# 16x16 blocks of a head's triangular inverse on VectorE by way of DMA, in a new order of the head rounds

## What is computed

```python
kk = einsum('cd,sd->cs', k, k)
a_mat = where(tri_strict, beta[:, None] * kk * decay, 0.0)
sol = triangular_solve(a_mat + eye, concat([v * beta, k * (beta * exp(G))]), lower=True, unit_diagonal=True)
value, k_cum = sol[..., :dv], sol[..., dv:]
for each chunk:                       # a recurrence over the chunks
    v_new = value - k_cum @ s
    o = q_dec @ s + attn_intra @ v_new
    s = s * chunk_decay + k_dec.T @ v_new
```

## Time and profile before

| | us |
|---|---|
| three runs | 2012.69, 2012.9, 2009.73 (median 2012.69) |
| the profiled execution | 2013.07 |
| its span, first to last instruction | 2011.3 |
| TensorE busy | 1960.4 (97% of the span) |
| VectorE, ScalarE, GpSimd busy | 905.4, 688.3, 931.0 |
| granted clock of TensorE, mean | 0.994 |

### The profile page before, as it was taken

How to read it: one execution, slowest core, us unless ns; L and a number is a source line. 1 busy time by engine, 2 the same in 40 slices (tenths; PEclk the granted TensorE clock), 3 DMA queues, 4 the chain that set the end, 5 groups by cost and what they waited for, 6 DMA issues and landing times.

```text
span 2011.3 us, 28269 instructions
## 1 busy us (share of the span) xinstructions
PE 1960.4 (97%) x10421; PEld 1600.4 (80%) x10421; DVE 905.4 (45%) x1567; ACT 688.3 (34%) x1383; POOL 931.0 (46%) x711
## 2 busy tenths in 40 slices
PE   7899999999999999999999999999999999999997
PEld 5787778877787888888888788888778888888886
DVE  4766776677652222121212356576532234335143
ACT  4333333333342223332324344544422332222122
POOL 3443354434444456444445533234244565646455
PEclk9999999999999999999999999999999999999998
DMA  5122212222222342323323322112142323323222
GB/s 190 54 85 73 73 27 78 83 63 63 65 72 84 121 157 92 105 95 94 98 92 102 117 84 74 52 63 74 53 136 85 107 80 105 105 84 100 92 101 73
DMA packets 52902, 178.50 MB, mean 89 GB/s; under 512 B 6688, under 2 KB 7520, under 8 KB 52576
## 3 DMA queue, kind: packets, MB, share of 16 engines
q1 hardware_dynamic: 52336, 174.88, 26.9%
q10 hardware_dynamic: 496, 2.65, 0.4%
HBM read 173.29 MB, written 4.23 MB: 88 GB/s over the span
## 4 chain that ended last, share of the span: by engine, by line
PE 93%; DVE 4%; issue 1%; ACT 1%; DMA 0%; POOL 0%; POOLq 0%; DVEq 0%; SPq 0%; ACTq 0%
PE bank L286 27%; PE bank L288 26%; PE bank L287 26%; PE bank L1515 2%; PE bank L1504 2%; PE bank L1498 2%; PE bank L974 1%; PE bank L1691 1%; PE bank L1678 1%; PE bank L958 1%; PE bank L944 1%; PE bank L918 0%; DMA residual<-x_t 0%; DVE raw_z L1893 0%; PE bank L1555 0%
## 5 line engine op out<-in xcount | busy, mean ns | idle before, releaser
L275 POOL TENSOR_TENSOR slab_lo<-slab_raw,slab_hi 128x512 fp32r<-128x512 f32 x604 | 824.2, 1389 | 977.7 <-ACT slab_hi L268 977.6
L286 PE MATMUL bank<-u_hi,slab_hi 128*128 128x512 f32 x1584 | 658.3, 416 | 21.9 <-POOL slab_lo L275 13.8
L288 PE MATMUL bank<-u_hi,slab_lo 128*128 128x512 f32 x1584 | 621.2, 392 | 0.0
L287 PE MATMUL bank<-u_lo,slab_hi 128*128 128x512 f32 x1584 | 619.6, 391 | 0.0
L268 ACT CAST slab_hi<-slab_raw 128x1024 fp32r<-128x1024 f32 x302 | 314.0, 1045 | 224.4 <-PE bank L288 223.3
L286 PEld LDWEIGHTS bank<-u_hi,slab_hi 128*128 128x128 f32 x1584 | 299.1, 189 | 85.7 <-issue 23.4
L288 PEld LDWEIGHTS bank<-u_hi,slab_lo 128*128 128x128 f32 x1584 | 298.3, 188 | 65.1
L287 PEld LDWEIGHTS bank<-u_lo,slab_hi 128*128 128x128 f32 x1584 | 299.7, 189 | 53.7 <-issue 1.9
L286 PE MATMUL bank<-hidden_hi,slab_hi 128*128 128x512 f32 x432 | 168.4, 390 | 0.3
L288 PE MATMUL bank<-hidden_hi,slab_lo 128*128 128x512 f32 x432 | 168.1, 389 | 0.0
L287 PE MATMUL bank<-hidden_lo,slab_hi 128*128 128x512 f32 x432 | 168.1, 389 | 0.0
(11 more groups left out here) (340 smaller groups left out, 2626.3 us busy)
## 6 DMA issues: line engine op xcount, KB each, us to landing
slab_raw<-slabs SPq DMA_DIRECT2D x302, 512.0 KB, 3.5
g_and_cum_rows<-row_store SPq DMA_DIRECT2D x7, 512.0 KB, 6.3
residual<-x_t SPq DMA_DIRECT2D x2, 1024.0 KB, 7.2
x_tok<-x SPq DMA_DIRECT2D x1, 2048.0 KB, 12.5
residual<-x_t SPq DMA_DIRECT2D x1, 2048.0 KB, 9.0
residual_store<-residual SPq DMA_DIRECT2D x1, 2048.0 KB, 10.0
residual<-residual_store ACTq DMA_DIRECT2D x1, 2048.0 KB, 8.8
out_t<-residual SPq DMA_DIRECT2D x8, 256.0 KB, 2.0
```

Source lines behind the costliest of these rows:

```text
L275: ins = pool.tensor_tensor(w_lo[s][:, ks, :], raw[s][:, ks, :], w_hi[s][:, ks, :].bitcast(F32), ALU.subtract)
L286: pe.matmul(bank, w_hi[s][:, k, :], x_hi[:, k, :], start=first, stop=False)
L287: pe.matmul(bank, w_hi[s][:, k, :], x_lo[:, k, :], start=False, stop=False)
L288: mm = pe.matmul(bank, w_lo[s][:, k, :], x_hi[:, k, :], start=False, stop=last)
```

## The change

The inverse's first levels leave TensorE. After `kk`, SP stores the masked matrix `a_t` to DRAM (`blocks_out`) and loads the 32 diagonal blocks of 16x16 back, one to a partition (`sub_u`, 32 partitions by 256). VectorE inverts all 32 blocks at once: `zb1` does sizes 2 and 4 in a few instructions on 8 to 16 elements and joins them to 8 (`join(4)`), `zb2` joins to 16 (`join(8)`). A join is two small matrix products, each one multiplication over all terms and a sum over the last axis. SP then stores the inverted blocks to a DRAM buffer that was zeroed once and loads the 64-wide diagonal halves back to `zi` (`blocks_back`). Levels 16, 32 and the last one stay on TensorE (`Y0` to `Y2`, `X0` to `X2`). GpSimd makes the two level masks over full tiles in one place (`am`). The masks of `kk` become one instruction. `ORDER` is rewritten: `fr` ahead of s0.0, `kpd` early, `zb1` and `zb2` around `S1`, and the steps from `xt` on later by up to some ten slab parts.

```diff
-LEVELS = 7
+SB = 16
+SUBS = T // SB
+DIAG = SB * (SB + 1)
+LEVELS = (16, 32)
 HB, QB = 64, 32
 HW = NT * HB
 SCALE = float(P) ** -0.5
 SLOTS = 4
-DVE_STEPS, LATE_STEPS = 26, 10
+DVE_STEPS, LATE_STEPS = 38, 10
...
     row_view = row_store.rearrange("(a h n) t -> h a (n t)", a=2, h=HEADS)
+    pitch = (P // SB) * SB * (P + 1)
+    a_store, z_store = [nc.dram_tensor(f"{x}_blocks_store", (NT * pitch,), F32, kind="Internal").ap() for x in "az"]
+
+    def tiles_in(store):
+        return store.rearrange("(n x) -> n x", n=NT)[:, 0:P * P].rearrange("n (p c) -> p n c", p=P)
+
+    def blocks_in(store):
+        return store.rearrange("(q x) -> q x", q=SUBS)[:, 0:SB * P].rearrange("q (i w) -> q i w", w=P)[:, :, 0:SB]
+
...
         kp, kd, vp = head("k_rhs", [P, T]), head("k_dec", [P, T]), head("v_rhs", [P, T])
-        a_c, a_off = a_t[:, 0:HW], a_t[:, HW:T]
-        a_levels, inv_prod = head("a_levels", [P, T]), head("inv_and_prod", [P, T])
-        atm = [a_levels[:, 0:HW], a_levels[:, HW:T]]
+        inv_prod = head("inv_and_prod", [P, T])
+        atm = [head(f"a_level{b}", [P, T]) for b in LEVELS]
+        sub_u, sub_z = [head(n, [SUBS, DIAG]) for n in ("blocks_u", "blocks_z")]
+        sub_p, sub_w = junk[0:SUBS, :], head("blocks_sums", [SUBS, 64])
         xi, yi = inv_prod[:, 0:HW], inv_prod[:, HW:T]
...
 
-        ORDER = """fvt s0.0 dif s0.1 colb fr bd s0.2 eg fk s0.3 kk th3 s0.4 S0 s0.5 z0 s0.6 xt sl3 E0 s0.7 dm qk s1.0 Y1
-                   e0 s1.1 tv P0 s1.2 vp s1.3 s1.4 X1 kpd T0 S1 s1.5 E1 s1.6 Y2 qd P1 s1.7 O0 s2.0 X2 e1 T1 S2 s2.1
-                   E2 cv0.0 s2.2 Y3 O1 s2.3 cv0.1 P2 X3 s2.4 cv0.2 s2.5 Y4 T2 s2.6 S3 cv0.3 s2.7 X4 E3 s3.0 e2 O2 s3.1 Y5
-                   th0 P3 s3.2 cv1.0 s3.3 X5 T3 cv1.1 s3.4 sl0 s3.5 Y6 O3 cv1.2 s3.6 tq s3.7 X6 cv1.3 s4.0 e3 s4.1 vk
-                   th1 s4.2 s4.3 r0 sl1 s4.4 r1 tfq s4.5 v1 cv2.0 s4.6 s4.7 r2 tk s5.0 v2 e4 s5.1 cv2.1 s5.2 r3 tfk
-                   s5.3 v3 cv2.2 s5.4 osq cv2.3 s5.5 s5.6 s5.7 on th2 s6.0 e5 s6.1 ot sl2 s6.2 oa s6.3 cola s6.4 colh
-                   s6.5 s6.6 s6.7 e6""".split()
+        ORDER = """fvt fr s0.0 dif s0.1 colb bd s0.2 eg fk s0.3 kk th3 s0.4 S0 s0.5 am s0.6 kpd E0 s0.7 dm qk s1.0 e0
+                   s1.1 tv P0 s1.2 vp zb1 T0 S1 s1.3 s1.4 zb2 E1 P1 s1.5 s1.6 qd s1.7 O0 s2.0 e1 s2.1 sl3 s2.2 T1 S2 s2.3
+                   E2 cv0.0 s2.4 O1 s2.5 cv0.1 P2 xt s2.6 cv0.2 s2.7 T2 s3.0 S3 Y0 e2 s3.1 cv0.3 E3 O2 s3.2 X0 s3.3 th0
+                   P3 cv1.0 s3.4 Y1 s3.5 T3 cv1.1 s3.6 X1 sl0 s3.7 O3 cv1.2 s4.0 Y2 e3 s4.1 tq cv1.3 s4.2 X2 th1 s4.3
+                   s4.4 vk s4.5 tfq sl1 s4.6 r0 cv2.0 s4.7 r1 s5.0 v1 e4 s5.1 cv2.1 tk s5.2 r2 s5.3 v2 cv2.2 s5.4 tfk s5.5
+                   r3 cv2.3 s5.6 v3 s5.7 osq th2 s6.0 e5 s6.1 s6.2 on sl2 cola s6.3 colh s6.4 ot s6.5 oa s6.6 s6.7
+                   e6""".split()
         LATE = {"cv0.0", "cv0.1", "cv0.2", "cv0.3", "cv1.0", "cv1.1", "cv1.2", "cv1.3", "cv2.0", "cv2.1", "cv2.2",
                 "cv2.3", "th0", "th1", "th2", "sl0", "sl1", "sl2", "tq", "tfq", "tk", "tfk", "cola", "colh"}
...
+            def blocks_out(c):
+                sp.wait_ge(sem("masked"), c + 1)
+                sp.wait_ge(sem("blocks_moved"), 80 * c + 32)
+                sp.dma_start(tiles_in(a_store), c4(a_t[:])).then_inc(sem("blocks_moved"), 16)
+                sp.wait_ge(sem("blocks_moved"), 80 * c + 48)
+                sp.dma_start(sub_u[:, 0:SB * SB].rearrange("q (i j) -> q i j", j=SB), blocks_in(a_store))\
+                    .then_inc(sem("blocks_moved"), 16)
+
+            def blocks_back(c):
+                sp.wait_ge(sem("sub_z"), c + 1)
+                sp.dma_start(blocks_in(z_store), sub_z[:, 0:SB * SB].rearrange("q (i j) -> q i j", j=SB))\
+                    .then_inc(sem("blocks_moved"), 16)
+                sp.wait_ge(sem("blocks_moved"), 80 * c + 80)
+                for r in (0, HB):
+                    sp.dma_start(c4(zi[r:r + HB, :]), tiles_in(z_store)[r:r + HB, :, r:r + HB])\
+                        .then_inc(sem("blocks_moved"), 16)
+
+            sp.wait_ge(sem("mhalf"), 1)
+            sp.dma_start(z_store[0:P * T].rearrange("(p t) -> p t", t=T), zeros[:]).then_inc(sem("blocks_moved"), 16)
+            sp.dma_start(z_store[P * T:].rearrange("(p t) -> p t", t=T), zeros[0:1, :]).then_inc(sem("blocks_moved"), 16)
+
...
                             if ph is ph_heads and j == 5:
+                                blocks_out(i - 1)
+                            if ph is ph_heads and j == 6:
+                                blocks_back(i - 1)
                                 load_rows(i)
                 else:
                     for j in range(ph.n):
                         load_slab(sp, ph, start, j)
+                        if ph is ph_gates and j == 5:
+                            blocks_out(HEADS - 1)
+                        if ph is ph_gates and j == 6:
+                            blocks_back(HEADS - 1)
             for m in range(KT):
                 sp.wait_ge(sem("result"), m + 1)
...
                 def level_y(l):
-                    if l < LEVELS - 1:
-                        pe.wait_ge(sem("atm"), 6 * c + l + 1)
-                    if l == 1:
-                        pe.wait_ge(sem("x0"), c + 1)
-                    else:
-                        pe.wait_ge(sem("x_new"), 5 * c + l - 1)
-                    if l < LEVELS - 1:
-                        quads(bA, atm[l % 2], xi).then_inc(sem("y_ps"), 1)
-                        return
+                    if l < len(LEVELS):
+                        pe.wait_ge(sem("atm"), 2 * c + l + 1)
+                    pe.wait_ge(sem("x_new"), 3 * c + l + 1)
                     pe.sem_inc(sem("level_begun"), 1)
                     for n in range(NT):
                         q = slice(n * HB, (n + 1) * HB)
-                        mm = pe.matmul(bA[HI, q], a_off[LO, q], xi[LO, q], start=True, stop=True)
+                        if l < len(LEVELS):
+                            for r in (LO, HI):
+                                mm = pe.matmul(bA[r, q], atm[l][r, n * P + r.start:n * P + r.stop], xi[r, q],
+                                               start=True, stop=True)
+                        else:
+                            mm = pe.matmul(bA[HI, q], a_t[LO, n * P + HB:(n + 1) * P], xi[LO, q], start=True, stop=True)
                     mm.then_inc(sem("y_ps"), 1)
 
                 def level_x(l):
-                    pe.wait_ge(sem("y"), 6 * c + l)
-                    if l == 1:
+                    pe.wait_ge(sem("y"), 3 * c + l + 1)
+                    if l == 0:
                         pe.wait_ge(sem("v_rhs"), c + 1)
-                    if l > 1:
-                        pe.wait_ge(sem("z_new"), 6 * c + l - 1)
-                    if l < LEVELS - 1:
-                        quads(bC, yi, zi).then_inc(sem("zy_ps"), 1)
-                        return
+                    else:
+                        pe.wait_ge(sem("z_new"), 3 * c + l)
                     pe.sem_inc(sem("level_begun"), 1)
                     for n in range(NT):
-                        mm = pe.matmul(bC[LO, n * HB:(n + 1) * HB], yi[HI, n * HB:(n + 1) * HB],
-                                       zf[HI, n * P + HB:(n + 1) * P], start=True, stop=True)
+                        q = slice(n * HB, (n + 1) * HB)
+                        if l < len(LEVELS):
+                            for r in (LO, HI):
+                                mm = pe.matmul(bC[r, q], yi[r, q], zi[r, q], start=True, stop=True)
+                        else:
+                            mm = pe.matmul(bC[LO, q], yi[HI, q], zf[HI, n * P + HB:(n + 1) * P], start=True, stop=True)
                     mm.then_inc(sem("zy_ps"), 1)
 
...
-                    for out_, p0, c0 in ((a_c, 0, 0), (a_c, HB, HB), (a_off, 0, HB)):
-                        p_, c_ = slice(p0, p0 + HB), slice(c0, c0 + HB)
-                        ins = dve.tensor_tensor(c4(out_[p_, :]), c4(bA[p_, :])[:, :, c_], c4(bdt[p_, :])[:, :, c_],
...
-                def z0():
-                    dve.wait_ge(sem("atm"), 6 * c + 1)
-                    dve.tensor_tensor(c4(zi[:]), half_tiles(level_mask[:, LEVELS - 1, :]), c4(atm[0]), ALU.subtract)\
-                        .then_inc(sem("z0"), 1)
+                one = "q (m x) -> q m x"
+
+                def square(x, b, at_):
+                    x = x[:].rearrange(one, m=SB // (2 * b))[:, :, at_:at_ + SB * b]
+                    return x.rearrange("q m (i w) -> q m i w", w=SB)[:, :, :, 0:b]
+
+                def product(b, left, right, out_, negate):
+                    m = SB // (2 * b)
+                    prod = sub_p[:, 0:m * b ** 3].rearrange("q (m i j k) -> q m i j k", m=m, i=b, j=b)
+                    for n in range(m):
+                        l_ = left[:, n].unsqueeze(2).to_broadcast([SUBS, b, b, b])
+                        r_ = right[:, n].rearrange("q k j -> q j k").unsqueeze(1).to_broadcast([SUBS, b, b, b])
```

(70 more changed lines are left out.)

29 lines of the change are left out of this document (14 added, 15 removed).

## The result

| | before | after |
|---|---|---|
| median of the runs, us | 2012.6 (2009.73 to 2012.90, 4 runs) | 2026.4 (2025.06 to 2028.49, 4 runs) |
| profiled execution, us | 2013.07 | 2028.49 |
| its span, us | 2011.3 | 2025.6 |
| mean granted clock | 0.994 | 0.985 |

The ratio is 1.0073, 95% interval 1.0061 to 1.0085: the change makes the kernel 0.7% slower, 14 us. The forecast was 2011, no difference; the time lies inside its range, near the upper end.

A forecast was written before the change was run, and what follows sets the result against it. TensorE, 93% of the span, was taken as the bound: -33.4 us for removed stages, +7 at round edges, +24.8 waits on VectorE, +0.4 for ot gave -1.2, so 2011 us; range 1994 to 2028.

The forecast's parts named there:

- the sum itself: Whole kernel: -33.4 + 7 + 24.8 + 0.4 = -1.2 us against the profiled 2013.07, giving 2011 us.
- the walk: VectorE's steps from kk to T2, priced stage by stage: TensorE waits 3.1 us a round, 24.8 in eight.
- T0 and T1: TensorE's first two transposes of the probabilities in a round: together wait 1.7 to 3.2 us for VectorE, 2.3 taken.
- The waits' sum: TensorE's added waits: 7 us at the round edges, 24.8 on VectorE, 0.4 at ot in the last round.
- T2: TensorE's next transpose of the probabilities after T1: waits 0.5 to 1.3 us a round for P2, 0.8 taken.
- the edge: Round's start, fr now before s0.0: TensorE waits 1.5 us for rsc, net +1.0, +7 us over seven edges.
- what left TensorE: Six of the inverse's twelve TensorE stages in a round go: 4.17 us a round saved, 33.4 in eight.
- a rival beside it: One or two block products a round blocked by GpSimd's splits: 1.3 us a round, 10 in eight, 2021 us; chance 0.17.
- The rule that I weighed: VectorE two-SBUF-input or fast-mode and GpSimd SBUF-reading instructions exclude each other, reductions don't: up to 1.5 us per block product.
- DMAs, queues, `zb1`: Blocks back at b+6.7 (b: kk's start), hidden with 1.3 to 1.8 us spare; queues cost nothing; zb1 takes 2.75 us.
- the rival of late blocks: Block DMAs land at b+11 (b: kk's start), delaying zb1: +2.3 us a round, +18 us, 2029 us; chance 0.16.

The follow-up runs named there:

- experiment 5: Kernel before the change with extra 128x512 VectorE products on a scratch tile ahead of P1 in each head round: 2051.8 us with three, 2064.4 with five.
- experiment 4: Changed kernel without the work of zb1 and zb2 (waits for the blocks, copies four columns; inverse not computed, all DMAs stay): 1983.7 us, ratio 0.9858.
- experiment 6: Changed kernel with the two 512-element products of zb2 over plain rows instead of repeated and strided operands (inverse not computed): 2010.9 us, ratio 0.9997.
- experiments 2: Changed kernel with 32 transposes of the identity ahead of TensorE's wait for the probabilities of T1, each of eight rounds: 2019.0 us, ratio 1.0031.
- 3: Changed kernel with the slab split of s2.0 on ScalarE and GpSimd carried out at s2.4 in rounds with a head: 2011.5 us, ratio 0.9995.

## Why the prediction was wrong, by its steps

**The step that failed is the sum itself: it has no term for the clock.** It priced a wait at its own length. The runs show that the long wait at T1 is followed by TensorE at half clock, and that this costs 14 to 17 us (experiment 5). With that the span closes: -36.8 (stages, experiment 4) + 34.1 (waits) + 14 to 17 (clock) = +11 to +14, measured +14.3. Forecast: -33.4 + 32.2 = -1.2. The missing term turned no change into 0.7% slower. The Trainium skill names the mechanism (page "TensorE: Matmul & The Clock Gate", section "What's actually happening"): the engine's default is the lower level, to which it returns after idling. The traces agree, with 0.50 from 226 us on here. It could have been weighed: before's own trace has the fall, in round 0, beside waits of 3.12 and 2.41 us, and the walk puts up to 3.2 us of wait on T0 and T1.

**The waits' sum, right to 2 us, is partly luck.** T0 and T1 waited some 12 us more in eight rounds than forecast, T2 some 5 less, the edge 1 less, and round 0's two waits shrank by 2.3, which the forecast had not counted. The next paragraphs take them one by one.

**Right: what left TensorE.** 4.17 a round forecast, 36.8 / 8 = 4.6 measured.

**Right: the edge.** Waits for `rsc` of 1.23 to 1.26 at seven edges where 1.5 was forecast, and 0.3 at the first; 9.1 less 3.3 = 5.8 us for 7, and undoing it gave 5.2.

**T0 and T1: mis-sized, above the upper bound.** 2.3 forecast, 3.2 at most, 0.56 + 3.29 = 3.85 measured. Two reasons in one place. A product of `zb2` was priced by a row over plain operands, 0.68; it takes 1.05. And it was put clear of the split of s2.0 in the sum, and only in a rival beside it; the split began at 223.09, ahead of the product of 223.14, which took 1.09 more. The rival priced that about right (1.3 a round), but without the clock, so its 2021 was 5 short. The rule that I weighed holds in the rows shown here: 2.14 for 1.05, 1.64 for 0.69 in experiment 5, the product begun first untouched in experiment 6, and the reduction at 225.31, beside the split's second half, at 0.67, its free price. By the Trainium skill's page "SBUF — State Buffer", section "Who interferes with whom", that is how it should be: exclusion is for a whole instruction, and reductions are not in it.

**T2: wrong in the loop, and right without the clock.** 0.8 forecast, none in rounds 1 to 7 and 1.03 in the last: TensorE came late itself, at half clock. With the clock kept up it waits 0.57 to 1.65 (experiments 2, 3 and 6, in 3 in the rounds without a half-clock stretch).

**Right: DMAs, queues, `zb1`.** `zb1` took 2.74 us (217.30 to 220.04) for 2.75 and waited for no landing; the rival of late blocks, which gave 2029, came within 3 us of the time by a cause that isn't there.

## What to carry over

A wait of TensorE can have two prices: its length, and a stretch at half clock beside and behind it. In rounds 1 to 8 of all these kernels that came with 24 of 26 waits of 3.2 to 3.3 us, with 7 of 14 of 2.1, and with none of 1.3 to 1.8. Those lengths are no safe bounds elsewhere: in round 0, where waits of 1.5 and 1.7 us stand less than 1 us apart, six kernels of seven have a stretch, and one wait of 1.8 us, in the second block, has one in five kernels of twelve. So what counts is how idle time is divided, not only its sum. Before work moves to an engine that has room on average, walk the densest stretch, price strided operands from strided rows, and look at what starts beside it on GpSimd. And where new work stands between a step and its reader, move the reader: the same work in another order, with two splits moved, went from 14 us slower to 31 us faster.
